# Differential attention with its scores in three banks, its output in two, and the memory keys and values moved behind it

## The chip, the cores and the metric

The kernel runs on one core of one Trainium2 chip. The metric is the device time of one execution in microseconds (us), less being better. TensorE (PE) multiplies, VectorE (DVE), ScalarE (ACT) and GpSimd (POOL) work on the results, and the queue of SyncE (SP) starts the weight loads. Every engine works through its own instructions in program order and waits on semaphores that the others raise.

## The reference, cut to what matters

Two transformer blocks on 512 tokens of width 1024. The change lies in the first block's mixer, which sums three gated branches:

```python
q_d, k_d, v_d, u_p, q_m, gate_logits = jnp.split(h @ w_in, split_pts, axis=-1)
# differential attention: 8 heads, two components of 64 each, blocks of 128 queries, causal
s = einsum(q, k) * scale + alibi_bias;  p = softmax(s)          # for each component c
a = p[:, :, 0] - lam * p[:, :, 1];      out = einsum(a, v)
y_attn = (rms_norm(out, subln_g) * (1 - lam_init)) @ w_attn_branch
y_pool = multiscale_pool(u_p, pool_w, pool_scale) @ w_pool_branch
k_m, v_m = split(rms_norm(mem, norm_mem) @ w_mem_kv)            # 256 memory tokens, 4 heads of 128
y_mem  = memory_cross_attention(q_m, k_m, v_m) @ w_mem_branch
mix = gates[0] * y_attn + gates[1] * y_pool + gates[2] * y_mem
```

## The kernel before

**Projections.** Every matrix product is done three times on PE, with weights and inputs each split into a high and a low part (`mm3`, L744; the instructions carry L747). Weights come in chunks of 512 KB through four places: SP loads a chunk, ACT rounds it (`act_round`, L687), POOL forms the rest (L728), and PE waits for that. A tile of 512 tokens with 8 contraction blocks is 24 matmuls, one with 4 blocks is 12.

**The differential stage** has 32 units, u = 4 e + i for head e and query block i, so unit u has (u mod 4) + 1 blocks of 128 keys. They go through the engines as a pipeline of steps s (`pe_diff`, `act_diff`, `dve_diff`). In step s:

- PE: the scores of unit s, a matmul for each of the two components (L1487); transposes of the combined probabilities of unit s-3 (L1495); the product with the values of unit s-4 into the output bank (L1503).
- DVE: the output of unit s-5, scaled (L1540); then for unit s-1 the bias and the maximum of each component (L1554), ahead of it at i = 0 a new scaling of the distances (L1551); then the combination of the two components of unit s-2 (L1562 to L1566).
- ACT: both exponentials of unit s-1 (L1515), the copy of the transposes of unit s-3 (L1523), the squares of unit s-6 (L1529).

The scores lie in four banks, two for each parity of s, so that the scores of unit s wait for the maxima of unit s-2. The output has one bank: the product of unit s-4 waits for the output of unit s-5 (`d_out(u - 1)`).

**Main work between the steps.** `weave` gives each engine, item by item, a piece of main work and then as many steps as are due by proportion; the pairing of items and steps is the same on all three engines. Main work is, in order: the gated pool branch `pg` (24 items: four times two gate tiles of two items each and two branch tiles of one item each), the memory queries `qm` (8 items), the normed memory `mem` (4 items, two transposed blocks each: PE L1637, ACT L1646, DVE L1658), the memory keys `km` (4) and the memory values `vm` (4). On DVE the item of a branch tile waits for that tile on PE and then runs L1598 and L1601; that of an even `qm` tile waits for the tile and copies it (L859). On ACT the item of a gate tile waits for it and runs a tanh, and the rounding of a later chunk stands behind it.

**Behind the stage** (`pe_branches`, `act_branches`, `dve_branches`): ACT takes roots (two table loads), DVE scales the 8 heads (L1753), PE does two gate tiles of `agt`; then PE turns the heads (L923, tiles `ao`) through two banks, ACT and DVE split them (L932, L942), and PE goes on with the branch tiles of `agt` and the memory attention.

Of the kernel before, what the change touches and what calls it, by code (L numbers as in the profile page):

```python
# [13 lines left out]
P = 128  # L14
# [150 lines left out]
def build(nc, a):  # L165
# [332 lines left out]
    d_scored = signal("d_scored", d_units)  # L498
    d_maxed = signal("d_maxed", d_units)
    d_exped = signal("d_exped", d_units)  # L500
# [56 lines left out]

    def in_ring(name, tiles, emptied, banks=(0, 1, 2, 3)):

        for u in range(tiles):  # L560
            b = banks[u % len(banks)]
# [909 lines left out]
    def d_bank(u, c):  # L1471
        return 2 + 2 * (u % 2) + c

    d_out_bank = bank(7, P)

    def pe_diff():
        PE.wait_ge(*freed_act("k", 7))
        PE.wait_ge(*freed_act("v", 15))
        PE.wait_ge(*mod_set(0, MOD_CHUNKS - 1))
        for s in range(N_D + 7):  # L1480
            if s < N_D:
                i, e, n = d_where(s)
                if s >= 2:
                    PE.wait_ge(*d_maxed(s - 2))
                for c in range(2):
                    part = slice(c * DIFF_DH, (c + 1) * DIFF_DH)
                    ins = PE.matmul(bank(d_bank(s, c), n), qT[part, e, i * P:(i + 1) * P], kT[part, e, 0:n])  # L1487
                ins.then_inc(*d_scored.by(s))
            if 0 <= s - 3 < N_D:
                u, (i, e, n) = s - 3, d_where(s - 3)  # L1490
                PE.wait_ge(*d_comb(u))
                if u >= 1:
                    PE.wait_ge(*d_copied(u - 1))
                for k in range(i + 1):
                    ins = PE.transpose(bank(6, P, k * P), sc2[u % 3][:, 0, k * P:(k + 1) * P], ident[:])  # L1495
                ins.then_inc(*d_turned.by(u))
            if 0 <= s - 4 < N_D:
                u, (i, e, n) = s - 4, d_where(s - 4)
                PE.wait_ge(*d_copied(u))
                if u >= 1:  # L1500
                    PE.wait_ge(*d_out(u - 1))
                for k in range(i + 1):
                    ins = PE.matmul(d_out_bank, aT[u % 2][:, k * P:(k + 1) * P], vt[:, k, e * P:(e + 1) * P],  # L1503
                                    start=k == 0, stop=k == i)
                ins.then_inc(*d_weighted.by(u))
            yield
# [143 lines left out]

    def dve_mem():
        DVE.wait_ge(*mixed("pg", 7))
        for b in range(CB):
            DVE.tensor_scalar(mdiag[:, b, :], ident[:], statistics("mem")[1][:, b:b + 1], None,
                              ALU.mult).then_inc(*diag.by("mem", b))
        for t in range(DT):
            DVE.wait_ge(*n_hi("mem", t))
# [4 lines left out]

    N_BESIDE_DIFF = 4 + 24 + 8 + 4 + 4 + 4

    def pe_beside_diff():
        yield from pe_gated_branch("pg", [(bhi, blo, SEQ)], 4, lambda: None, lambda n, k: PE.wait_ge(*pool_lo(k)))
        yield from pe_gemm("qm", X)
        yield from pe_mem()
        yield from pe_gemm("km", M, ready=lambda n, k: PE.wait_ge(*n_lo("mem", k)))
        yield from pe_gemm_tokens("vm", TOKENS["vm"])  # L1670

    def act_beside_diff():
        yield from act_gated_branch("pg")
        yield from act_copied("qm")
        yield from act_mem()
        yield from act_copied("km")
        yield from act_tokens("vm", vm)

    def dve_beside_diff():
        yield from dve_gated_branch("pg")  # L1680
        yield from dve_copied("qm")
        yield from dve_mem()
        yield from dve_copied("km")
        yield from dve_tokens("vm", vm)

    def pe_diff_stage():
        run(pe_pool())
        weave(pe_beside_diff(), pe_diff(), N_BESIDE_DIFF - 4, N_D + 7)

    def act_diff_stage():  # L1690
        run(act_pool())
        weave(act_beside_diff(), act_diff(), N_BESIDE_DIFF - 4, N_D + 7)

    def dve_diff_stage():
        for b in range(CB):
            DVE.wait_ge(*rstd("mem", b))
# [9 lines left out]
    def pe_branches():  # L1706
        def before(s):
# [7 lines left out]

        PE.wait_ge(*d_maxed(N_D - 1))
        PE.wait_ge(*d_copied(N_D - 1))
        at = pe_gated_branch("agt", [(ahi, alo, SEQ)], DT, lambda: pe_token_to_split(
            "ao", lambda t, k: qT[:, t, k * P:(k + 1) * P], DT, lambda t: head_scaled(t)),
            lambda n, k: PE.wait_ge(*ts_lo("ao", k)))  # L1720
# [3 lines left out]
        run(pe_gated_branch("mg", [(bhi, blo, SEQ)], 4, lambda: pe_token_to_split(  # L1724
            "om", lambda t, k: om[:, k, t * P:(t + 1) * P], MEM_HEADS, lambda t: attended("mem", 15)),
            lambda n, k: PE.wait_ge(*ts_lo("om", k))))

    def act_branches():
        ACTE.wait_ge(*d_squared(N_D - 1))
        ACTE.activation(hrms, hs, ACT.Sqrt, scale=1.0 / P, bias=eps).then_inc(*head_rms.by(0))  # L1730
        ACTE.preload_act_table(ACT.Exp)
        at = act_gated_branch("agt", before_branch=lambda: act_token_to_split("ao", ahi, DT, subg))
        for _ in range(5):
# [10 lines left out]

        run(act_gated_branch("mg", split, lambda: act_token_to_split("om", bhi, MEM_HEADS)))

    def dve_branches():
        DVE.wait_ge(*head_rms(0))
        dve_step(DVE.reciprocal(hs, hrms))
        dve_after()  # L1750
        for e in range(DIFF_HEADS):
# [3 lines left out]
        at = dve_gated_branch("agt", before_branch=lambda: dve_token_to_split("ao", ahi, alo, DT, subg))  # L1755
        for _ in range(5):
# [7 lines left out]

        run(dve_gated_branch("mg", split, lambda: dve_token_to_split("om", bhi, blo, MEM_HEADS)))

# [1169 lines left out]
```

## Time and profile before

| | us |
|---|---|
| median of three runs | 1913.64 (1910.06 to 1914.26) |
| profiled execution, its own time | 1917.37 |
| its span, first to last instruction | 1916.1 |
| PE busy | 1765.5 (92% of the span) |
| DVE, ACT, POOL busy | 1009.2, 744.4, 576.0 |
| mean granted TensorE clock | 0.962 |

The differential stage with its main work runs from about 206 to 403 us of the span, the turning of the heads from 412 to 421. Busy time is per engine; a number in square brackets behind a row is idle time of that engine just ahead of it, and what ended it.

### The profile page before, as it was taken

Reading aid. Unit: us, or ns where it says so; the run is one execution under the profiler, and the core shown is the slowest. Engines: PE = TensorE matmul, PEld = TensorE weight load, DVE = VectorE, ACT = ScalarE, POOL = GpSimd, SP = SyncE. Lnnn points to the kernel's source line nnn. Section 1 sums busy time; section 2 is a strip of 40 time slices with the busy share of each in tenths; the row PEclk is TensorE's granted clock in tenths of the full one; section 3 lists DMA queues with packets and bytes.
Section 4 is the critical chain, followed back from the end, with each engine's and each line's share of the span. In section 5 each row is a group of like instructions: output and inputs, shape, how many; then the busy total and the mean of one; then the engine's idle time right before and its main releaser. Section 6 shows DMA issues by size and latency. Waiting matters only on the chain.

```text
span 1916.1 us, 24709 instructions
## 1 busy us (share of the span) xinstructions
PE 1765.5 (92%) x9464; PEld 1408.1 (73%) x9464; DVE 1009.2 (53%) x2024; ACT 744.4 (39%) x1460; POOL 576.0 (30%) x257
## 2 busy tenths in 40 slices
PE   7999999889999899999998899898889979998887
PEld 5879767678888688887887676555568857885675
DVE  3678545542242533443787415566643577965533
ACT  4222344543233444444223341566633143224532
POOL 3566221253344044444343021100012224421131
PEclk9999999999999799999998799999999989999988
DMA  7456212132234133333653021000002423221021
GB/s 221 132 153 184 77 52 59 45 110 67 82 95 132 34 89 98 99 99 108 197 157 88 1 85 44 23 1 1 2 12 85 125 69 97 83 59 34 25 75 44
DMA packets 255363, 155.25 MB, mean 81 GB/s; under 512 B 5969, under 2 KB 250894, under 8 KB 255246
## 3 DMA queue, kind: packets, MB, share of 16 engines
q1 hardware_dynamic: 251998, 147.12, 26.2%
q10 hardware_dynamic: 3248, 6.55, 1.0%
q8 instruction: 76, 1.25, 0.3%
q14 instruction: 41, 0.34, 0.1%
HBM read 151.55 MB, written 2.10 MB: 80 GB/s over the span
## 4 chain that ended last, share of the span: by engine, by line
PE 81%; DVE 9%; ACT 5%; issue 3%; DMA 0%; DVEq 0%; SPq 0%; ACTq 0%
PE ps L747 64%; PE ps L2172 3%; PE ps L2161 3%; DVE mod_sums L1436 2%; PE ps L2191 2%; ACT probs L2245 2%; PE ps L960 1%; PE ps L1503 1%; PE ps L1451 1%; PE ps L1487 1%; PE ps L1015 1%; DVE probsT L2272 1%; DVE probs L2260 1%; DVE h_lo L1050 1%; ACT w_hi L687 1%
## 5 line engine op out<-in xcount | busy, mean ns | idle before, releaser
L728 POOL TENSOR_TENSOR w_lo<-w_raw,w_hi 128x1024 fp32r<-128x1024 f32 (+1 forms) x220 | 535.0, 2435 | 1263.6 <-ACT w_hi L687 1263.3
L747 PE MATMUL ps<-h_hi,w_lo 128*128 128x512 f32 x1088 | 440.3, 405 | 22.7 <-DVE h_lo L1050 9.7
L747 PE MATMUL ps<-h_lo,w_hi 128*128 128x512 f32 x1088 | 429.4, 395 | 0.0
L747 PE MATMUL ps<-h_hi,w_hi 128*128 128x512 f32 x1088 | 429.1, 394 | 0.0
L747 PEld LDWEIGHTS ps<-h_hi,w_lo 128*128 128x128 f32 x1088 | 207.6, 191 | 83.7 <-issue 19.2
L687 ACT ACTIVATE w_hi<-w_raw 128x1024 fp32r<-128x1024 f32 (+1 forms) x220 | 228.4, 1043 | 41.2 <-PE ps L747 34.4
L747 PEld LDWEIGHTS ps<-h_hi,w_hi 128*128 128x128 f32 x1088 | 207.7, 191 | 44.9
L747 PEld LDWEIGHTS ps<-h_lo,w_hi 128*128 128x128 f32 x1088 | 208.2, 191 | 42.0 <-issue 1.4
L1436 DVE SCALAR_TENSOR_TENSOR mod_sums<-mod_raw,small,mod_sums 128x256 f32<-128x256 f32 x336 | 182.9, 618 | 0.0
L2172 PE MATMUL ps<-ident,probs 128*128 128x128 f32 x528 | 86.6, 289 | 37.5 <-ACT probs L2245 15.6
L2172 PEld LDWEIGHTS ps<-ident,probs 128*128 128x128 f32 x528 | 56.8, 143 | 78.7 <-ACT probs L2245 31.8
L1881 DVE SCALAR_TENSOR_TENSOR conv<-ps,cols,conv 128x511 f32<-128x511 f32 x44 | 33.0, 750 | 125.3 <-ACT conv L1844 125.3
L2245 ACT ACTIVATE probs<-probs,small 128x512 f32<-128x512 f32 (+3 forms) x128 | 93.3, 729 | 12.0 <-DVE small L2260 9.0
L2234 ACT ACTIVATE probsT<-ps 128x256 f32<-128x256 f32 (+2 forms) x128 | 48.5, 379 | 106.7 <-PE ps L2172 106.5
L2632 DVE SCALAR_TENSOR_TENSOR ps<-u_T,cols,ps 128x512 f32<-128x512 f32 x116 | 76.8, 744 | 0.0
L747 PE MATMUL ps<-f_hi,w_lo 128*128 128x512 f32 x176 | 71.1, 404 | 4.6 <-DVE f_lo L1891 4.6
L747 PE MATMUL ps<-f_hi,w_hi 128*128 128x512 f32 x176 | 69.8, 397 | 0.0
L747 PE MATMUL ps<-f_lo,w_hi 128*128 128x512 f32 x176 | 69.3, 394 | 0.0
L1433 DVE SCALAR_TENSOR_TENSOR mod_sums<-mod_raw,small 128x256 f32<-128x256 f32 x48 | 59.8, 1285 | 7.0 <-DMA mod_raw<-in_mod_w 6.9
L2272 DVE COPY probsT<-ps 128x256 f32<-128x256 f32 (+2 forms) x128 | 55.8, 436 | 12.1 <-PE ps L2172 11.6
L747 PE MATMUL ps<-c_hi,w_lo 128*128 128x256 f32 x192 | 56.4, 293 | 1.7 <-DVE c_lo L1050 1.7
L747 PE MATMUL ps<-w_lo,h_hi 128*128 128x256 f32 x192 | 55.5, 289 | 0.6 <-POOL w_lo L728 0.6
(406 smaller groups left out, 3247.9 us busy)
## 6 DMA issues: line engine op xcount, KB each, us to landing
w_raw<-in_w_in SPq DMA_DIRECT2D x56, 512.0 KB, 6.4
mod_raw<-in_mod_w SPq DMA_DIRECT2D x24, 1024.0 KB, 5.2
w_raw<-in_w_up SPq DMA_DIRECT2D x44, 512.0 KB, 3.8
w_raw<-in_od_w_in SPq DMA_DIRECT2D x28, 512.0 KB, 3.8
w_raw<-in_ev_w_in SPq DMA_DIRECT2D x20, 512.0 KB, 3.8
w_raw<-in_w_down SPq DMA_DIRECT2D x16, 512.0 KB, 4.0
w_raw<-in_w_mem_kv SPq DMA_DIRECT2D x8, 512.0 KB, 4.0
w_raw<-in_w_attn_branch SPq DMA_DIRECT2D x8, 512.0 KB, 4.0
```

The source lines that it names most:

```text
L687: ACTE.activation(whi[:, p, 0:n], raw[:, p, 0:n], ACT.Copy).then_inc(*chunk_hi.by(c))
L728: POOL.tensor_tensor(wlo[:, p, 0:n], raw[:, p, 0:n], f(whi[:, p, 0:n]), ALU.subtract).then_inc(*chunk_lo.by(c))
L747: ins = PE.matmul(out, l, r, start=first and n == 0, stop=last and n == 2)
L1433: dve_step(DVE.scalar_tensor_tensor(out, w[:, k, :], c, zero1.to_broadcast([P, MOD_COLS]), ALU.mult, ALU.add))
L1436: ins = DVE.scalar_tensor_tensor(out, w[:, k, :], c, out, ALU.mult, ALU.add)
L2161: ins = PE.matmul(ps[:, pair_bank(s) * 512 + off:pair_bank(s) * 512 + off + w], u["q"][s], u["k"][s][:, at:at + w])
L2172: ins = PE.transpose(bank(b, P, k * P), probs[s][p % 2][:, at:at + P], ident[:])
L2191: PE.matmul(ps[s * HEAD:(s + 1) * HEAD, b * 512 + lo:b * 512 + hi], u0["v"](k, s), probsT[s][g % 2][:, k, lo:hi], start=n == 0, stop=n == ...
L2234: ACTE.activation(turned_to(probsT, p - 1, s, u["act"]), bank(5, w).rearrange("p (k n) -> p k n", n=P), ACT.Copy).then_inc(*p_copied_act.b ...
L2245: ins = ACTE.activation(S, S, ACT.Exp, bias=neg_max[:, s:s + 1], scale=-1.0, accum_out=total[:, s:s + 1])
L2272: DVE.tensor_copy(turned_to(probsT, p, s, part), bank(4, len(part) * P).rearrange("p (k n) -> p k n", n=P)).then_inc(*p_copied_dve.by(x_, ...
L2632: dve_step(DVE.scalar_tensor_tensor(so_far, src, wcol, so_far_, ALU.mult, ALU.add))
```

## The change

- The scores use three banks by component: component c of unit s lies in bank 2 + (2 s + c) mod 3. The scores of unit s wait for the maximum of component 0 of unit s-1 (the signal of the maxima now has an event for each component).
- The output uses two banks, 7 and 5 in turn; the product of a unit waits for the output two units before.
- DVE does the output of unit s-5 behind the maxima of unit s-1.
- `mem` is interleaved with `qm` (two items of `qm`, one of `mem`, four times), and `km` and `vm` leave the main work, which now has 36 items instead of 44 for the same 39 steps.
- Behind the stage PE does `km`, then `vm` with two head turns behind each tile, then `agt`. The turns go through four banks. ACT and DVE have their pieces in the matching order.

```diff
-    in_ring("qm", 4, by_table("qm"), TWO)
-    in_ring("mem", 8, lambda u: [n_lo("mem", u)], TWO)
+    for u in range(4):
+        in_ring("qm", 1, by_table("qm"), (u % 2,), u)
+        in_ring("mem", 2, lambda t: [n_lo("mem", t)], (1 - u % 2, u % 2), 2 * u)
-    in_ring("ao", 8, lambda u: [ts_lo("ao", u)], (2, 3))
+    in_ring("ao", 8, lambda u: [ts_lo("ao", u)], (2, 3, 4, 5))
...
     def d_bank(u, c):
-        return 2 + 2 * (u % 2) + c
-    d_out_bank = bank(7, P)
+        return 2 + (2 * u + c) % 3
+    def d_out_bank(u):
+        return bank((7, 5)[u % 2], P)
...
             if s < N_D:
-                if s >= 2:
-                    PE.wait_ge(*d_maxed(s - 2))
+                if s >= 1:
+                    PE.wait_ge(*d_maxed(s - 1, 0))
...
-                if u >= 1:
-                    PE.wait_ge(*d_out(u - 1))
+                if u >= 2:
+                    PE.wait_ge(*d_out(u - 2))
...
         for s in range(N_D + 7):
-            if 0 <= s - 5 < N_D:
-                u, (i, e, n) = s - 5, d_where(s - 5)
-                DVE.wait_ge(*d_weighted(u))
-                DVE.tensor_scalar(qT[:, e, i * P:(i + 1) * P], d_out_bank, d_stats(u)[:, 4:5], None,
-                                  ALU.mult).then_inc(*d_out.by(u))
             if 0 <= s - 1 < N_D:
...
-                ins.then_inc(*d_maxed.by(u))
+                    ins.then_inc(*d_maxed.by(u, c))
+            if 0 <= s - 5 < N_D:
+                u, (i, e, n) = s - 5, d_where(s - 5)
+                DVE.wait_ge(*d_weighted(u))
+                DVE.tensor_scalar(qT[:, e, i * P:(i + 1) * P], d_out_bank(u), d_stats(u)[:, 4:5], None,
+                                  ALU.mult).then_inc(*d_out.by(u))
...
-    N_BESIDE_DIFF = 4 + 24 + 8 + 4 + 4 + 4
+    N_BESIDE_DIFF = 24 + 8 + 4
+    def queries_and_memory(queries, memory):
+        for u in range(4):
+            next(queries)
+            yield
+            next(queries)
+            yield
+            next(memory)
+            yield
...
     def pe_beside_diff():
         yield from pe_gated_branch("pg", [(bhi, blo, SEQ)], 4, lambda: None, lambda n, k: PE.wait_ge(*pool_lo(k)))
-        yield from pe_gemm("qm", X)
-        yield from pe_mem()
-        yield from pe_gemm("km", M, ready=lambda n, k: PE.wait_ge(*n_lo("mem", k)))
-        yield from pe_gemm_tokens("vm", TOKENS["vm"])
+        yield from queries_and_memory(pe_gemm("qm", X), pe_mem())
...
-        weave(pe_beside_diff(), pe_diff(), N_BESIDE_DIFF - 4, N_D + 7)
+        weave(pe_beside_diff(), pe_diff(), N_BESIDE_DIFF, N_D + 7)
...
+        run(pe_gemm("km", M, ready=lambda n, k: PE.wait_ge(*n_lo("mem", k))))
+        turn = pe_token_to_split("ao", lambda t, k: qT[:, t, k * P:(k + 1) * P], DT, lambda t: head_scaled(t))
+        for _ in pe_gemm_tokens("vm", TOKENS["vm"]):
+            next(turn)
+            next(turn)
```

## Rows read from the trace of the kernel before

**Rows 1.** The page: busy us, share of the span, instructions.

```profile
PE 1765.5 (92%) x9464; PEld 1408.1 (73%) x9464; DVE 1009.2 (53%) x2024; ACT 744.4 (39%) x1460; POOL 576.0 (30%) x257
```

**Rows 2.** Stretches: us; PE, PEld, DVE, ACT, POOL busy; granted clock, DMA share, GB/s.

```profile
206.30:428.75 222.45, 203.81 (x1109) 155.32 (x1109) 109.01 (x321) 109.72 (x293) 68.13 (x29) 0.98 0.23 66
257.60:261.00 3.40, 3.40 (x11) 2.61 (x11) 1.78 (x7) 2.08 (x7) 0.00 (x0) 0.53 0.52 154
371.80:375.20 3.40, 3.40 (x26) 3.06 (x28) 0.65 (x3) 0.69 (x1) 2.39 (x1) 1.00 0.00 0
1718.60:1725.30 6.70, 5.53 (x16) 2.97 (x13) 2.32 (x7) 2.26 (x6) 0.27 (x1) 0.51 0.26 78
1851.70:1855.10 3.40, 3.40 (x9) 2.64 (x9) 0.24 (x1) 0.00 (x0) 2.37 (x1) 0.52 0.04 12
```

**Rows 3.** Waits of PE, 206.3 to 428.75: total us, times, longest.

```profile
PE ps L1503 <- DVE q_T L1540: 9.4, 9, 1.5
PE ps L923 <- DVE a_lo L942: 3.5, 3, 1.4
PE ps L1495 <- ACT diff_aT L1523: 2.0, 2, 1.0
```

**Rows 4.** Timeline of PE (start, us) around the end of a branch tile.

```profile
254.67 0.40 PE L747 MATMUL ps<-b_hi,w_hi 128*128 128x512 f32 x1
255.00 0.49 PE L1487 MATMUL ps<-k_T,q_T 64*128 64x128 f32 x4
...
257.39 0.46 PE L1503 MATMUL ps<-v_tok,diff_aT 128*128 128x128 f32 x2 [1.53 <-DVE q_T L1540]
```

**Rows 5.** Timeline of DVE behind the same tile and the next one.

```profile
255.11 0.69 DVE L1598 SCALAR_TENSOR_TENSOR gate_p<-gate_p,ps 128x512 f32<-128x512 f32 x1 [8.01 <-PE ps L747]
255.83 1.16 DVE L1601 TENSOR_SCALAR mix_T<-gate_p 128x512 f32<-128x512 f32 x1
256.91 0.34 DVE L1540 TENSOR_SCALAR q_T<-ps,small 128x128 f32<-128x128 f32 x1
257.17 0.68 DVE L1554 CUSTOM_DVE_ANT_0 diff_s<-ps,distance 128x512 f32<-128x512 f32 x1
...
263.57 0.48 DVE L1551 TENSOR_SCALAR distance<-distance,small 128x512 f32<-128x512 f32 x1
264.08 0.29 DVE L1554 CUSTOM_DVE_ANT_0 diff_s<-ps,distance 128x128 f32<-128x128 f32 x1
```

**Rows 6.** The chain that ended last: a branch tile (start, us).

```profile
239.76 2.75 PE ps L747 x12
```

**Rows 7.** Operations: count, ns min/median/max, first and last start.

```profile
L1601 DVE TENSOR_SCALAR mix_T<-gate_p x8: 426/792/2119, 230.1 to 319.6; 128x512 f32<-128x512 f32 x8
L859 DVE TENSOR_SCALAR qm_T<-ps x2: 691/692/692, 328.0 to 344.3; 128x512 f32<-128x512 f32 x2
L1646 ACT ACTIVATE m_hi<-ps,small,cols x8: 547/552/564, 356.8 to 371.0; 128x256 fp32r<-128x256 f32 x8
L1658 DVE SCALAR_TENSOR_TENSOR m_lo<-ps,cols,m_hi x8: 483/484/485, 357.4 to 371.6; 128x256 fp32r<-128x256 f32 x8
```

**Rows 8.** Groups by form, 212 to 429: busy us, mean ns; idle before.

```profile
L728 POOL TENSOR_TENSOR w_lo<-w_raw,w_hi 128x1024 fp32r<-128x1024 f32 x28 | 67.1, 2404 | 152.8 <-ACT w_hi L687 152.6
L687 ACT ACTIVATE w_hi<-w_raw 128x1024 fp32r<-128x1024 f32 x28 | 29.3, 1051 | 2.9 <-PE ps L747 2.9
L1515 ACT ACTIVATE diff_s<-diff_s,small 128x384 f32<-128x384 f32 x16 | 9.7, 607 | 15.8 <-DVE small L1554 15.8
```

**Rows 9.** Timeline of PE: the last memory item, the first of km.

```profile
368.94 1.06 PE L1637 MATMUL ps<-m_diag,mem_in 128*128 128x128 f32 x8
371.70 0.35 PE L747 MATMUL ps<-m_hi,w_lo 128*128 128x256 f32 x1 [1.71 <-issue]
```

**Rows 10.** Timeline of PE: the gaps ahead of the last two stretches.

```profile
1717.19 0.65 PE L2172 MATMUL ps<-ident,probs 128*128 128x128 f32 x4 [2.12 <-ACT probs L2245]
1851.45 0.51 PE L747 MATMUL ps<-o_hi,w_lo 128*128 128x512 f32 x1 [1.82 <-DVE o_lo L2797]
```

More of the change, by code:

```diff
@@ L498, in build @@
     d_scored = signal("d_scored", d_units)
-    d_maxed = signal("d_maxed", d_units)
+    d_maxed = signal("d_maxed", [(u, c) for u in d_units for c in range(2)])
     d_exped = signal("d_exped", d_units)
@@ L556, in build, with in_ring @@
     BANK, BEFORE, EMPTIED, holder = {}, {}, {}, {}
-    def in_ring(name, tiles, emptied, banks=(0, 1, 2, 3)):
-        for u in range(tiles):
-            b = banks[u % len(banks)]
+    def in_ring(name, tiles, emptied, banks=(0, 1, 2, 3), first=0):
+        for u in range(first, first + tiles):
+            b = banks[(u - first) % len(banks)]
             BANK[name, u], BEFORE[name, u] = b, holder.get(b)
@@ L1499, in pe_diff @@
                 PE.wait_ge(*d_copied(u))
-                if u >= 1:
-                    PE.wait_ge(*d_out(u - 1))
+                if u >= 2:
+                    PE.wait_ge(*d_out(u - 2))
                 for k in range(i + 1):
-                    ins = PE.matmul(d_out_bank, aT[u % 2][:, k * P:(k + 1) * P], vt[:, k, e * P:(e + 1) * P],
+                    ins = PE.matmul(d_out_bank(u), aT[u % 2][:, k * P:(k + 1) * P], vt[:, k, e * P:(e + 1) * P],
                                     start=k == 0, stop=k == i)
@@ L1655, in dve_mem @@
                               ALU.mult).then_inc(*diag.by("mem", b))
+    def dve_mem():
         for t in range(DT):
@@ L1661, in dve_mem @@
                 yield
-    N_BESIDE_DIFF = 4 + 24 + 8 + 4 + 4 + 4
+    N_BESIDE_DIFF = 24 + 8 + 4
+    def queries_and_memory(queries, memory):
+        for u in range(4):
+            next(queries)
+            yield
+            next(queries)
+            yield
+            next(memory)
+            yield
+        assert next(queries, None) is None and next(memory, None) is None
     def pe_beside_diff():
         yield from pe_gated_branch("pg", [(bhi, blo, SEQ)], 4, lambda: None, lambda n, k: PE.wait_ge(*pool_lo(k)))
-        yield from pe_gemm("qm", X)
-        yield from pe_mem()
-        yield from pe_gemm("km", M, ready=lambda n, k: PE.wait_ge(*n_lo("mem", k)))
-        yield from pe_gemm_tokens("vm", TOKENS["vm"])
+        yield from queries_and_memory(pe_gemm("qm", X), pe_mem())
     def act_beside_diff():
         yield from act_gated_branch("pg")
[L1674 to L1677, printed above, removed]
+        ACTE.wait_ge(*tile_done("pg", 15))
+        yield from queries_and_memory(act_copied("qm"), act_mem())
     def dve_beside_diff():
         yield from dve_gated_branch("pg")
[L1681 to L1684, printed above, removed]
+        dve_mem_diag()
+        yield from queries_and_memory(dve_copied("qm"), dve_mem())
     def pe_diff_stage():
         run(pe_pool())
-        weave(pe_beside_diff(), pe_diff(), N_BESIDE_DIFF - 4, N_D + 7)
+        weave(pe_beside_diff(), pe_diff(), N_BESIDE_DIFF, N_D + 7)
     def act_diff_stage():
         run(act_pool())
-        weave(act_beside_diff(), act_diff(), N_BESIDE_DIFF - 4, N_D + 7)
+        weave(act_beside_diff(), act_diff(), N_BESIDE_DIFF, N_D + 7)
     def dve_diff_stage():
@@ L1723, in pe_branches @@
         weave(at, pe_attention("mem", mem_units, mprobs, mprobsT, before), 27, 20)
-        run(pe_gated_branch("mg", [(bhi, blo, SEQ)], 4, lambda: pe_token_to_split(
-            "om", lambda t, k: om[:, k, t * P:(t + 1) * P], MEM_HEADS, lambda t: attended("mem", 15)),
+        run(pe_gated_branch("mg", [(bhi, blo, SEQ)], 4, lambda: run(pe_token_to_split(
+            "om", lambda t, k: om[:, k, t * P:(t + 1) * P], MEM_HEADS, lambda t: attended("mem", 15))),
             lambda n, k: PE.wait_ge(*ts_lo("om", k))))
@@ L1731, in act_branches @@
         ACTE.preload_act_table(ACT.Exp)
-        at = act_gated_branch("agt", before_branch=lambda: act_token_to_split("ao", ahi, DT, subg))
+        run(act_copied("km"))
+        split = act_token_to_split("ao", ahi, DT, subg)
+        for _ in act_tokens("vm", vm):
+            next(split)
+            next(split)
+        at = act_gated_branch("agt")
         for _ in range(5):
@@ L1743, in split @@
                 ACTE.activation(ahi[:, t, :], mixT[:, t, :], ACT.Copy).then_inc(*mx_hi.by(t))
-        run(act_gated_branch("mg", split, lambda: act_token_to_split("om", bhi, MEM_HEADS)))
+        run(act_gated_branch("mg", split, lambda: run(act_token_to_split("om", bhi, MEM_HEADS))))
     def dve_branches():
@@ L1750, in dve_branches @@
         dve_after()
+        keys = dve_copied("km")
         for e in range(DIFF_HEADS):
@@ L1754, in dve_branches @@
                               ALU.mult).then_inc(*head_scaled.by(e))
-        at = dve_gated_branch("agt", before_branch=lambda: dve_token_to_split("ao", ahi, alo, DT, subg))
+            if e % 2:
+                next(keys)
+        split = dve_token_to_split("ao", ahi, alo, DT, subg)
+        for _ in dve_tokens("vm", vm):
+            next(split)
+            next(split)
+        at = dve_gated_branch("agt")
         for _ in range(5):
@@ L1763, in split @@
             DVE.tensor_tensor(alo[:, t, :], mixT[:, t, :], f(ahi[:, t, :]), ALU.subtract).then_inc(*mx_lo.by(t))
-        run(dve_gated_branch("mg", split, lambda: dve_token_to_split("om", bhi, blo, MEM_HEADS)))
+        run(dve_gated_branch("mg", split, lambda: run(dve_token_to_split("om", bhi, blo, MEM_HEADS))))
     def pe_mix():
```

13 lines of the change are left out of this document (5 added, 8 removed).

## The prediction

> **What bounds the kernel now.** The page first: PE is busy 92% of the span, no other engine more than 53% [rows 1]. Another engine's time matters only where PE stands still for it, or where such standing makes PE's clock fall. The change adds and removes almost no PE instruction, so the question is what becomes of PE's idle time in the stretch that it touches. That stretch, 206.3 to 428.75 us (pool products to the first memory scores), has 222.45 us with 203.81 busy, thus 18.6 idle [rows 2], of which 1.9 belong to the pool products, which the change leaves alone. Next the waits of PE: 9.4 us in nine waits of the value product (L1503) for the output step, 2.0 of the transposes for ACT's copy, 3.5 for the split of the turned heads [rows 3], and 1.7 ahead of the first `km` matmul [rows 9]; sum 16.6 us.
>
> How a wait of the first kind arises is seen at one branch tile. Its last matmul ends at 255.07; PE does the scores and the transposes and then stands 1.53 us for the output [rows 4]. DVE had to take the branch tile first: L1598 from 255.11, L1601 from 255.83, the output from 256.91, ended at 257.25, and PE starts 0.14 later [rows 4, 5]. The scores and transposes, some 0.8 us here, cover part of DVE's delay. And the first maximum of the unit scored one step earlier starts only at 257.17 [rows 5], over 2 us after PE has begun to score the next unit at 255.00. Before, nobody minds: the scores wait for the unit two back. The gap is followed by a clock of 0.53 for 3.4 us, the 1.2 GHz level, against 1.00, the 2.4 GHz level, elsewhere [rows 2]. Such a stretch under a busy PE costs half its length, 1.7 us. The 0.98 over the whole 222 us [rows 2] is two of them, together 3.4 us.
>
> **What the change removes.** The output wait, by two banks: 9.4 us. ACT's late copy, 2.0, which stands behind late maxima and moves into the terms below. The turned heads wait, 1.4 at the longest [rows 3], because two banks are filled, split and freed in turn; with four banks and a `vm` tile behind every second head (24 matmuls of half width, so the 2.75 us of 12 full ones [rows 6]) they wait no more: 3.5. The 1.7 ahead of `km` go into a new term. With the two slow stretches, 16.6 + 3.4 = 20.0 us are taken out, and all that comes back is counted anew.
>
> **What it adds: the scores wait for unit s-1.** With three banks, the scores of s need component 0 of s-1 out of its bank. That maximum is in DVE's step s, behind DVE's main item; PE's scores of s are the very first thing behind PE's main item. Where DVE's main item waits for the tile that PE has just ended (all eight branch tiles, `qm` 0), nothing of PE's covers DVE's way: 0.04 to start, 0.72 from L1598 to the next, L1601, the maximum, 0.14 back to PE [rows 4, 5]. L1601 lasts 0.43 at the least and 2.1 at the most [rows 7]: 0.35 to the next instruction for the second tile of each pair, about 1.5 for the first, over which POOL's 2.4 us operation on a weight chunk lies [rows 8]. Nothing in the change moves that chunk from there, so I keep 1.5. The maximum lasts 0.29 for 128 keys and 0.68 for 512 [rows 5], about 0.42 and 0.55 between. At i = 0 scaling the distances adds 0.51 [rows 5].
>
> Pairing 36 items with 39 steps, item n (from 0) has step floor(39(n+1)/36) - 1 as its last. First tiles are items 4, 10, 16, 22 with steps 4, 10, 17, 23, so the maxima are of units 3 (512 keys), 9 (256), 16 (128 and the scaling), 22 (384): gaps of 3.1, 2.8, 3.2, 3.0. Second tiles, items 5, 11, 17, 23 (units 4, 10, 17, 23): 2.1, 1.8, 1.7, 1.9. Sum 19.6 us. Items 11 and 23 have two steps at once: for unit 11 DVE must do maximum, output and combination (about 1.6 us) and another 0.68 and 0.14, against 2.2 us of work on PE: 0.2; for unit 24 it needs 2.9 against 1.1: 1.8. Together 2.0.
>
> At gate items DVE waits for nothing of PE's main item, and a gate half has 2.75 us of matmuls in which the maximum gets done: no gap. At `qm` 0 the copy takes 0.69 [rows 7] (0.60 to the next), the maximum 0.55, the ends 0.18: 1.3 us. At `qm` 2 no scores are left.
>
> **Memory items.** Two have scores behind them (items 26 and 29). PE's own work in one is 1.06 us [rows 9]; then ACT has to do two m_hi of 0.55 and DVE the last m_lo of 0.48 [rows 7] ahead of the maximum. ACT comes late besides: for the first it has two exponentials of 0.6 [rows 8] behind DVE's copy of `qm` 0, for the second its own copy of `qm` 1, the rounding of 1.05 [rows 8] and two exponentials. Followed through, PE stands 1.9 and 2.7 us. The third costs 0.3 (combination of unit 31). Ahead of `km`, in place of the 1.7, the last m_lo pair comes behind `qm` 3's copy, a rounding and squares on ACT: 2.2. For `km` and `vm` PE has eight times 2.75, 22 us of matmuls, which hide the roots, two table loads and the head scaling; if they did not, that is if DVE freed the bank of `km` 0 late, 1 us more. One weight chunk of `vm` is 0.8 late. Sum of these: 7.9 us.
>
> All new gaps: 19.6 + 2.0 + 1.3 + 7.9 = 30.8 us, against 16.6 removed: 14.2 more.
>
> **The clock.** The trace of before shows gaps on both sides of the point where the clock falls: after 1.71 it stays [rows 2, 9], after 1.53 and 1.82 it falls for 3.4 us, after 2.12 for 6.7 [rows 2, 4, 10]. Of the new gaps eleven places have between 1.7 and 3.2 us, ten of them 1.8 or more. Bounds: none falls, 0; each falls for 6.7 us, 11 x 3.4 = 37 us. I take ten falls of 3.4 us, most of it under a busy PE, 1.6 us each: 16, less the 3.4 there are now: 12.6. The rows with gaps of 1.8 and more are nearest, and there the clock fell.
>
> The Trainium skill weighs this otherwise: its page "TensorE: Matmul & The Clock Gate", section "Why this matters for your kernels", lets only gaps longer than nearly all of those forecast here drop the clock. This case's trace disagrees, by the gaps of 1.53 and 1.82. By that rule the sum would lack the whole term of 16; what the time would be without it is the first rival.
>
> **Sum.** 14.2 + 12.6 = 26.8 us. The profiled execution took 1917.4 (span 1916.1 and 1.3 around it), so it would be near 1944; that run lies 3.7 above the median of 1913.6. On the median: 1940.
>
> **Rivals.**
> - The clock holds: new gaps as above, hardly a fall: 14.2 - 3.4 = 10.8, time 1924. For it: the gap of 1.71 that left it at 1.00, and only two falls from the waits of [rows 3]. Against: the rows of 1.53 and up.
> - The falls run together, as after the 2.12 gap, or L1601 of the first tiles takes its 2.1 each time: 12 to 15 us more, 1954.
> - Faster: the maxima are in time. If DVE came to component 0 before PE's main item ends at branch tiles and `qm` 0, the 19.6, 2.0 and 1.3 would be nothing, and with them nearly all falls of the clock: 7.9 - 20.0 = -12, time 1902. It decides when the scores' waits at these items average below 0.5 us. For it: at all gate items DVE is early. Against: the maximum that starts at 257.17 [rows 5] belongs to the unit that this wait would ask for at 255.0; output first or second changes 0.27 us of this.
> - The two waits balance: PE pays at the scores what it paid at the product, no change. It needs gaps at branch tiles no longer than the 1.5 at most of now, though the scores and transposes that covered them come to stand behind the wait.
>
> **How the numbers follow.** Main case 0.64 (1931 to 1948 by itself, five to thirteen falls), clock holds 0.15, falls run together 0.11, balance 0.04, faster 0.06. About 0.2%, 3.8 us, is what a measurement of this kernel can tell from no change. Leaving out balance, faster and the outer tails: 1921 to 1954. Slower 0.90, same 0.04, faster 0.06.
>
> **What would show it.** In the profile after: PE's wait at L1487 for DVE's maxima (L1554), some twelve times and 20 to 28 us in total, near zero now; L1503's wait for L1540 gone; no wait at L923; gaps of about 3 us behind first branch tiles and 2 us behind second ones; a granted clock of the stage clearly below the 0.98 of [rows 2]. I am wrong if the scores' waits sum to under 10 us, or if the clock stays at 1.00 after gaps of 2 to 3 us.

## The result, and the profile after

The changed kernel takes 1935.25 us (median of four runs, 1928.92 to 1940.59) against 1913.95 (four runs beside it, 1910.06 to 1916.74). The ratio is 1.0107, with a 95% interval from 1.0086 to 1.0127: slower by 21.3 us. (The ratios here and below are the recorded ones with their intervals; the quotient of two medians comes out 0.0003 to 0.0008 higher, less than half an interval.) Forecast were 1940 (1921 to 1954) and slower with a chance of 0.90. The profiled run took 1940.59 us with a span of 1939.2, which is 23.1 more than before. It is the slowest of the four, 5.3 us above their median, as the profiled run of before was 3.4 above its own, so the profiles overstate the difference by some 2 us.

In this kernel L1492 are the scores, L1500 the transposes, L1508 the product with the values, L1554 the maxima, L1551 the scaling of the distances, L1571 the combination, L1603 and L1606 the two operations of a branch tile, L748 the matmuls and L729 POOL's operation.

The page's row of busy time, which answers to [rows 1]. The amount of work is the same:

```profile
PE 1776.3 (92%) x9464; PEld 1417.4 (73%) x9464; DVE 1017.9 (52%) x2024; ACT 745.7 (38%) x1460; POOL 574.0 (30%) x257
```

The waits of PE from 206 to 446 us (total us, times, longest), which answer to [rows 3]:

```profile
PE ps L1492 <- DVE small L1554: 26.7, 12, 4.1
PE ps L748 <- DVE m_lo L1664: 1.6, 1, 1.6
PE ps L748 <- POOL w_lo L729: 1.2, 1, 1.2
PE ps L1620 <- DVE b_lo L1633: 1.0, 1, 1.0
PE ps L748 <- DVE b_lo L1633: 0.9, 1, 0.9
PE ps L1500 <- DVE diff_s L1571: 0.5, 1, 0.5
PE ps L1642 <- ACT qm_T L853: 0.3, 1, 0.3
```

The product's wait for the output and the turned heads' wait for their split are gone. In their place the scores wait twelve times for the maxima. The two waits for b_lo belong to the pool products and were there before.

The stretches (us; PE, PEld, DVE, ACT and POOL busy; granted clock, DMA share, GB/s), which answer to [rows 2]. The first is the whole stage. It starts, as in [rows 2], 0.76 us ahead of the first pool product and ends at the first memory scores. The others are single places in it.

```profile
208.03:450.85 242.82, 210.57 (x1110) 161.40 (x1110) 116.79 (x321) 110.73 (x293) 69.43 (x29) 0.94 0.21 60
234.60:241.30 6.70, 5.62 (x18) 4.52 (x19) 2.55 (x8) 1.79 (x5) 0.14 (x1) 0.52 0.37 112
244.90:248.20 3.30, 3.30 (x14) 2.91 (x13) 2.58 (x10) 2.00 (x8) 0.00 (x0) 0.53 0.00 0
272.20:275.50 3.30, 3.30 (x14) 2.86 (x12) 0.00 (x0) 1.02 (x5) 0.00 (x0) 0.53 0.37 111
279.20:282.60 3.40, 3.40 (x22) 2.31 (x23) 3.29 (x13) 2.31 (x8) 0.00 (x0) 1.00 0.00 0
306.30:313.00 6.70, 5.73 (x19) 4.40 (x20) 2.39 (x9) 1.66 (x7) 0.30 (x1) 0.52 0.32 93
342.00:345.40 3.40, 3.40 (x21) 2.41 (x18) 1.08 (x6) 1.76 (x7) 0.00 (x0) 1.00 0.51 149
350.70:354.00 3.30, 2.89 (x12) 2.24 (x13) 2.93 (x15) 2.15 (x10) 0.00 (x0) 0.53 0.02 5
368.10:371.50 3.40, 3.40 (x19) 2.84 (x20) 3.23 (x15) 2.73 (x10) 0.00 (x0) 1.00 0.00 0
381.40:384.70 3.30, 3.17 (x10) 1.67 (x11) 2.21 (x11) 1.87 (x7) 0.00 (x0) 0.54 0.54 162
```

The stage is 242.82 us long instead of 222.45, so 20.4 more. Its idle time is 242.82 - 210.57 = 32.25 instead of 18.64 (13.6 more), and its busy time 210.57 instead of 203.81 (6.8 more). The stage also starts 1.7 us later (the first pool product is at 208.79 instead of 207.06). That shift lies ahead of the change: it was 0.7 to 2.6 us in the experiments. Behind the stage 1.0 us is left of the 23.1. Six times the clock falls to the 1.2 GHz level, for some 27 us together instead of 6.8.

The timeline of PE at every wait of over 1 us from the first branch tile on (start, us; in brackets the idle time ahead of it):

```profile
235.68 0.80 PE L1492 MATMUL ps<-k_T,q_T 64*128 64x128 f32 x4 [3.23 <-DVE small L1554]
244.25 0.70 PE L1492 MATMUL ps<-k_T,q_T 64*128 64x256 f32 x4 [1.97 <-DVE small L1554]
270.92 0.92 PE L1492 MATMUL ps<-k_T,q_T 64*128 64x384 f32 x4 [2.74 <-DVE small L1554]
279.18 1.13 PE L1492 MATMUL ps<-k_T,q_T 64*128 64x512 f32 x4 [1.72 <-DVE small L1554]
307.27 1.22 PE L1492 MATMUL ps<-k_T,q_T 64*128 64x256 f32 x4 [4.05 <-DVE small L1554]
316.05 0.92 PE L1492 MATMUL ps<-k_T,q_T 64*128 64x384 f32 x4 [1.58 <-DVE small L1554]
341.63 1.13 PE L1492 MATMUL ps<-k_T,q_T 64*128 64x512 f32 x4 [2.71 <-DVE small L1554]
348.52 0.49 PE L1492 MATMUL ps<-k_T,q_T 64*128 64x128 f32 x4 [1.85 <-DVE small L1554]
351.11 1.23 PE L1492 MATMUL ps<-k_T,q_T 64*128 64x256 f32 x4 [1.50 <-DVE small L1554]
363.12 1.13 PE L1492 MATMUL ps<-k_T,q_T 64*128 64x512 f32 x4 [1.26 <-DVE small L1554]
368.08 0.49 PE L1492 MATMUL ps<-k_T,q_T 64*128 64x128 f32 x4 [1.79 <-DVE small L1554]
381.53 2.01 PE L1492 MATMUL ps<-k_T,q_T 64*128 64x512 f32 x4 [2.29 <-DVE small L1554]
404.34 0.35 PE L748 MATMUL ps<-m_hi,w_lo 128*128 128x256 f32 x1 [1.64 <-DVE m_lo L1664]
417.10 0.38 PE L748 MATMUL ps<-w_lo,m_hi 128*128 128x256 f32 x1 [1.22 <-POOL w_lo L729]
```

The first eight are the eight branch tiles in order, followed by the second step at one of them (351.11), `qm` 0 (363.12) and the two memory items that have scores behind them. The longest gap, 4.05 us, is at the third first tile. There DVE (first fence) and POOL (second) did this:

```profile
303.25 0.69 DVE L1603 SCALAR_TENSOR_TENSOR gate_p<-gate_p,ps 128x512 f32<-128x512 f32 x1 [4.77 <-PE ps L748]
303.97 0.43 DVE L1606 TENSOR_SCALAR mix_T<-gate_p 128x512 f32<-128x512 f32 x1
304.32 2.56 DVE L1551 TENSOR_SCALAR distance<-distance,small 128x512 f32<-128x512 f32 x1
306.91 0.29 DVE L1554 CUSTOM_DVE_ANT_0 diff_s<-ps,distance 128x128 f32<-128x128 f32 x1
```

```profile
301.15 2.41 POOL L729 TENSOR_TENSOR w_lo<-w_raw,w_hi 128x1024 fp32r<-128x1024 f32 x1 [7.41 <-ACT w_hi L688]
304.06 2.53 POOL L729 TENSOR_TENSOR w_lo<-w_raw,w_hi 128x1024 fp32r<-128x1024 f32 x1 [0.50 <-ACT w_hi L688]
```

L1606 began 0.09 us ahead of POOL's second operation and took 0.43. The scaling behind it came under the second one and took 2.56 instead of the 0.48 of [rows 5].

### The profile page after: what moved, and what is told of

The parts are those of the page before. It is cut to its first block, busy times and chain, and to the rows that moved or that the text cites. A ratio compares the mean times of both kernels' runs of the same rounds, so it can differ in the third digit from the quotient of the medians.

```text
span 1939.2 us, 24707 instructions
## 1 busy us (share of the span) xinstructions
PE 1776.3 (92%) x9464; PEld 1417.4 (73%) x9464; DVE 1017.9 (52%) x2024; ACT 745.7 (38%) x1460; POOL 574.0 (30%) x257
## 3 DMA queue, kind: packets, MB, share of 16 engines
q8 instruction: 76, 1.25, 0.3%
## 4 chain that ended last, share of the span: by engine, by line
PE 81%; DVE 10%; ACT 5%; issue 3%; POOL 0%; DMA 0%; DVEq 0%; SPq 0%; ACTq 0%
PE ps L748 63%; PE ps L2197 3%; PE ps L2186 3%; DVE mod_sums L1440 3%; PE ps L2216 2%; ACT probs L2270 2%; PE ps L1492 1%; PE ps L964 1%; PE ps L1508 1%; PE ps L1455 1%; DVE probsT L2297 1%; PE ps L1019 1%; PE ps L1500 1%; DVE probs L2285 1%; DVE h_lo L1054 1%
## 5 line engine op out<-in xcount | busy, mean ns | idle before, releaser
L729 POOL TENSOR_TENSOR w_lo<-w_raw,w_hi 128x1024 fp32r<-128x1024 f32 (+1 forms) x220 | 533.0, 2426 | 1290.4 <-ACT w_hi L688 1290.3
L748 PE MATMUL ps<-h_hi,w_lo 128*128 128x512 f32 x1088 | 442.6, 407 | 22.2 <-DVE h_lo L1054 9.7
L748 PE MATMUL ps<-h_lo,w_hi 128*128 128x512 f32 x1088 | 431.2, 396 | 0.0
L748 PE MATMUL ps<-h_hi,w_hi 128*128 128x512 f32 x1088 | 430.5, 396 | 0.0
L748 PEld LDWEIGHTS ps<-h_hi,w_lo 128*128 128x128 f32 x1088 | 208.8, 192 | 83.6 <-issue 19.7
L748 PEld LDWEIGHTS ps<-h_hi,w_hi 128*128 128x128 f32 x1088 | 208.8, 192 | 45.5
L748 PEld LDWEIGHTS ps<-h_lo,w_hi 128*128 128x128 f32 x1088 | 209.4, 192 | 41.9 <-issue 1.4
L748 PE MATMUL ps<-f_hi,w_lo 128*128 128x512 f32 x176 | 70.7, 401 | 4.6 <-DVE f_lo L1916 4.6
L748 PE MATMUL ps<-f_hi,w_hi 128*128 128x512 f32 x176 | 69.7, 396 | 0.0
L748 PE MATMUL ps<-f_lo,w_hi 128*128 128x512 f32 x176 | 69.3, 394 | 0.0
L2297 DVE COPY probsT<-ps 128x256 f32<-128x256 f32 (+2 forms) x128 | 55.8, 436 | 12.1 <-PE ps L2197 11.6
L748 PE MATMUL ps<-c_hi,w_lo 128*128 128x256 f32 x192 | 56.5, 294 | 2.1 <-DVE c_lo L1054 1.9
L748 PE MATMUL ps<-c_hi,w_hi 128*128 128x256 f32 x192 | 55.5, 289 | 0.0
```

Source lines behind the costliest of these rows:

```text
L729: POOL.tensor_tensor(wlo[:, p, 0:n], raw[:, p, 0:n], f(whi[:, p, 0:n]), ALU.subtract).then_inc(*chunk_lo.by(c))
L748: ins = PE.matmul(out, l, r, start=first and n == 0, stop=last and n == 2)
L2297: DVE.tensor_copy(turned_to(probsT, p, s, part), bank(4, len(part) * P).rearrange("p (k n) -> p k n", n=P)).then_inc(*p_copied_dve.by(x_, ...
```

## The experiments

Eight kernels ran. Every ratio is against the kernel before on the same chip, whose median was 1917.39 us (13 runs) beside the first four and 1915.68 (19 runs) beside the last four. "The stage" is the time from the first pool product to the first memory scores, in the profiled run. It was 221.7 us before and 242.1 after.

| | what it is | median | ratio, 95% | stage | scores' waits |
|---|---|---|---|---|---|
| e1 | after, with the old banks and order | 1917.44 | 0.9993, 0.9982 to 1.0004 | 220.5 | 0.7 |
| e2 | before, with the new banks and order | 1937.34 | 1.0096, 1.0081 to 1.0111 | 239.2 | 27.1 |
| e3 | after, maxima of unit s in step s | 1903.81 | 0.9925, 0.9909 to 0.9942 | 207.0 | 3.9 |
| e4 | after, gaps filled with matmuls | 1928.45 | 1.0051, 1.0033 to 1.0069 | 230.5 | 8.8 |
| e5 | after, L1606 behind the maxima | 1924.11 | 1.0036, 1.0022 to 1.0050 | 228.6 | 19.0 |
| e6 | before, maxima of unit s in step s | 1914.56 | 0.9990, 0.9976 to 1.0004 | 219.0 | none |
| e7 | e2, maxima of unit s in step s | 1905.61 | 0.9940, 0.9921 to 0.9960 | 211.6 | 1.0 |
| e8 | e3, scaling ahead of its step | 1902.01 | 0.9926, 0.9911 to 0.9941 | 208.0 | 3.0 |

### e1 and e2: which half of the change costs

The change has two halves that don't need each other: the banks with their waits and DVE's order, and the moved memory work with the four-bank head turns. e1 takes the banks out of the kernel after. e2 puts them alone into the kernel before. This is e1's edit against the kernel after; the step's output in DVE also goes ahead of the maxima again. e2's edit against the kernel before is its reverse.

```diff
-        return 2 + (2 * u + c) % 3
+        return 2 + 2 * (u % 2) + c
...
-                if s >= 1:
-                    PE.wait_ge(*d_maxed(s - 1, 0))
+                if s >= 2:
+                    PE.wait_ge(*d_maxed(s - 2, 1))
...
-                if u >= 2:
-                    PE.wait_ge(*d_out(u - 2))
+                if u >= 1:
+                    PE.wait_ge(*d_out(u - 1))
```

> The changed kernel with its four old score banks, its one output bank and the output ahead of the maxima; the interleaved memory items and the keys and values behind the attention stay. Theory A (the scores' wait for the unit just before is the cost): the 26.7 us of PE's waits at the scores are gone, the waits of the value product for the output come back with 9 to 12 us, the turned heads don't wait; time 1905 to 1917, at or a little below the kernel before. Rival B (the moved memory work costs the time, by its late chunks and its chain through ACT and DVE): the time stays at 1925 or more, with the waits at the memory items and ahead of km and vm.

> The kernel before with only the banks changed: scores through three banks, two output banks, output behind the maxima; the memory work stays where it was. Theory A: waits at the scores of 22 to 32 us in total behind the eight branch tiles, two memory query tiles and four memory items, the output waits of 9.4 us gone, four to nine stretches of low clock in the stage; time 1928 to 1942. Rival B: 1917 or less, since the banks remove a wait.

Measured: e1 is level with before (0.9993) and e2 has the loss (1.0096, where the whole change has 1.0107). The waits of PE from 206 to 446 us, first of e1 (L1507 is the product, L1544 the output), then of e2 (L1488 are the scores, L1550 the maxima):

```profile
PE ps L1507 <- DVE q_T L1544: 8.8, 10, 1.6
```

```profile
PE ps L1488 <- DVE small L1550: 27.1, 13, 3.4
PE ps L923 <- DVE a_lo L942: 3.2, 3, 1.4
```

With the old banks the old output wait is back and the scores hardly wait (0.7). With the new banks alone the scores wait 27.1 us and the turned heads still 3.2. So the loss is the scores' wait, and the moved memory work, which by itself is no gain that these runs can tell, is not its cause. In e1's profile it takes away the 3.5 us of the turned heads, puts 1.6 ahead of `km` and 1.6 ahead of a weight chunk of `vm`, and the transposes wait 3.3 us for ACT's copy where it was 2.0 before. The place of the output on DVE, behind the maxima or ahead of them, was moved together with the banks in both kernels, so its own share isn't shown.

### e3: the same banks, the maxima one step earlier

Theory: nothing but DVE's order makes the scores late. In step s the scores of unit s wait for a maximum that DVE takes in its own step s, behind its main item. If DVE does the maxima of unit s last in step s, they are done ahead of the next main item, on which it waits for PE anyway. The body of the maxima is moved whole, from the head of the step to its end.

```diff
         for s in range(N_D + 7):
-            if 0 <= s - 1 < N_D:
-                u, (i, e, n) = s - 1, d_where(s - 1)
...
             if 0 <= s - 5 < N_D:
...
             if 0 <= s - 2 < N_D:
...
+            if s < N_D:
+                u, (i, e, n) = s, d_where(s)
...
             yield
```

> The changed kernel with one thing moved on DVE: in step s it does the maxima of unit s, last in the step, in place of those of unit s-1, so they stand ahead of the next main item. Theory A (only DVE's order makes the scores wait): scores' waits under 4 us in total, idle time of PE in the stage 5 to 10 us in place of 30, at most two stretches of low clock there; time 1895 to 1905, faster than the kernel before. Rival C (DVE's way is simply too long for this pipeline, and the wait goes elsewhere, to the combination or the output): waits of 10 us or more at the transposes or products, time 1912 or more.

Measured: 1903.81, ratio 0.9925, below both kernels. The waits of PE, and the whole stage in the columns of the stretches above:

```profile
PE ps L1492 <- DVE small L1569: 3.9, 4, 2.2
```

```profile
208.93:416.67 207.74, 198.14 (x1110) 152.77 (x1109) 116.36 (x321) 109.92 (x293) 69.67 (x29) 1.00 0.24 71
```

The clock is 1.00 throughout, PE idles for 9.6 us instead of 32.25, and it is busy for 198.14 us instead of 210.57, with the same number of matmuls. DVE's timeline at the first branch tile shows the order (L1569 are now the maxima):

```profile
230.72 0.69 DVE L1569 CUSTOM_DVE_ANT_0 diff_s<-ps,distance 128x512 f32<-128x512 f32 x1 [2.49 <-PE ps L1500]
...
233.38 0.69 DVE L1603 SCALAR_TENSOR_TENSOR gate_p<-gate_p,ps 128x512 f32<-128x512 f32 x1 [1.35 <-PE ps L748]
234.10 1.88 DVE L1606 TENSOR_SCALAR mix_T<-gate_p 128x512 f32<-128x512 f32 x1
```

PE begins the next scores at 233.28. The maximum that they need was begun at 230.72, in time in which DVE would have waited for the tile. L1606 takes as long as ever and nobody waits for it here.

### e4: what of the loss is clock

Theory: part of the loss isn't the gaps themselves but the clock behind them. e4 keeps PE at work in the gaps with 103 matmuls of 384 columns, put ahead of the scores' wait; their results go to a free part of an output bank and are read by nobody. The wait for the output that the next product into this bank needs anyway is put ahead of them.

```diff
+    FILL = {4: 13, 10: 13, 17: 13, 23: 13, 5: 7, 11: 7, 18: 7, 24: 7, 25: 7, 27: 4, 28: 4, 31: 8}
...
+                if s in FILL and s >= 6:
+                    PE.wait_ge(*d_out(s - 6))
+                for _ in range(FILL.get(s, 0)):
+                    PE.matmul(ps[:, (7, 5)[s % 2] * 512 + P:(7, 5)[s % 2] * 512 + 512], hhi[:, 0, 0:P], hhi[:, 0, 0:3 * P])
                 if s >= 1:
                     PE.wait_ge(*d_maxed(s - 1, 0))
```

> The changed kernel with useless matmuls of 384 columns on PE ahead of the scores that wait: 13 at the four first branch tiles, 4 to 8 at the eight other places, 17 us in total, less than the gaps. They write columns that nobody reads. Theory A (the low clock behind the gaps costs some 10 us of the 21): the low clock in the stage goes from 27.3 us to under 10, scores' waits from 26.7 to about 9, the rest unchanged; time 1924 to 1930. Rival D (the clock term is nothing, the gaps alone are the loss): no change against the changed kernel, 1935, or more where a filler is longer than its gap.

Measured: 1928.45, ratio 1.0051. The stage, and PE at the first of the filled gaps (the first line shows the last nine of its thirteen useless matmuls):

```profile
208.88:440.13 231.25, 216.45 (x1212) 170.29 (x1212) 116.59 (x321) 110.58 (x293) 70.13 (x29) 1.00 0.22 64
```

```profile
233.82 1.73 PE L1493 MATMUL ps<-h_hi 128*128 128x384 f32 x9
236.58 0.49 PE L1498 MATMUL ps<-k_T,q_T 64*128 64x128 f32 x4 [1.03 <-DVE small L1560]
```

The useless matmuls cost 216.45 - 198.14 = 18.3 us (against the busy time of e3), and 8.8 of waiting is left. Together that is 27.1, as long as the 26.7 of gaps in the kernel after. The clock stays at 1.00 and the stage is 11.6 us shorter. So with the same delay at the scores, a clock that doesn't fall is worth 11.6 us in the profile and 1.0107 - 1.0051, some 10.7 us, in the times. With the intervals of the two ratios the latter is good to 5 us or so.

### e5: L1606 out of the way

Theory: each gap is a sum of DVE's operations, with L1606 as one term. e5 halves the tile only behind the maxima of the step, so the term should vanish from the branch gaps and from nothing else. The rival: DVE is late for another reason, and the gaps stay.

```diff
             if job == "pg":
-                ins = DVE.tensor_scalar(mixT[:, fm, :], g, 0.5, None, ALU.mult)
+                later.append((fm, g))
+                return
...
                     ins.then_inc(*d_maxed.by(u, c))
+            while later:
+                fm, g = later.pop()
+                DVE.tensor_scalar(mixT[:, fm, :], g, 0.5, None, ALU.mult).then_inc(*mixed.by("pg", fm))
```

> The changed kernel with one DVE operation per branch tile moved: the halved product (the operation that took 1.4 to 1.8 us behind first branch tiles and 0.43 behind second ones) comes behind the maxima of the step, not ahead of them. Theory A (the gap is DVE's way from tile to maximum, term by term): the eight gaps at branch tiles shrink by 1.3 us each at three of the first and 0.35 at the others, scores' waits from 26.7 to about 20; with fewer low-clock stretches time 1926 to 1932 where the changed kernel has 1935. Rival E (GpSimd's operation holds up whatever DVE does there next, the scaling of the distances or the maximum, so that moving one operation wins nothing): waits of 25 or more, 1935.

Measured: 1924.11, ratio 1.0036. The first five gaps at branch tiles:

```profile
234.61 0.49 PE L1492 MATMUL ps<-k_T,q_T 64*128 64x128 f32 x4 [1.51 <-DVE small L1556]
240.10 0.70 PE L1492 MATMUL ps<-k_T,q_T 64*128 64x256 f32 x4 [1.64 <-DVE small L1556]
263.67 0.92 PE L1492 MATMUL ps<-k_T,q_T 64*128 64x384 f32 x4 [1.25 <-DVE small L1556]
269.99 1.13 PE L1492 MATMUL ps<-k_T,q_T 64*128 64x512 f32 x4 [1.38 <-DVE small L1556]
295.88 0.70 PE L1492 MATMUL ps<-k_T,q_T 64*128 64x256 f32 x4 [1.63 <-DVE small L1556]
```

3.23, 1.97, 2.74 and 1.72 became 1.51, 1.64, 1.25 and 1.38. The first tiles lose the long L1606, the second tiles its 0.35. At the third first tile 4.05 became 1.63, a gain of 2.4 us where the theory had 0.35. Without L1606 ahead of it the scaling began at 295.01, 0.09 us before POOL's operation, and took 0.49; the halving, now behind the maxima, was held up in its place (2.05 us) and nobody waited for it. So the largest single gain came from a tenth of a microsecond in POOL's start. The recorded rival, that POOL holds up whatever comes next, is refuted for the maximum: at the first tile it ran at 233.86 under POOL's pair of operations (230.67 to 235.40) and took its usual 0.69. For the scaling this run doesn't test it. All eight gaps sum to 11.6 instead of 19.9 us; two other waits grew by 0.3 each. The scores' waits sum to 19.0 instead of 26.7, and the stage is 13.5 us shorter. The other 5.8 are nearly all less busy time of PE (204.78 instead of 210.57 us): the clock falls three times instead of six. It stayed at 1.00 behind all five of these gaps.

### e6, e7 and e8: which parts of e3 are needed

e6 puts e3's order into the kernel before. e7 puts it into e2, so that it has the new banks but the memory work where it was. Their diffs move the same body as e3's. e8 is e3 with the scaling of the distances moved from the head of a step i = 0 to behind the last maxima of the step before; this is its edit against e3.

```diff
-                if i == 0:
+                if s == 0:
                     dve_step(DVE.tensor_scalar(dist[:], dist[:], slopes[:, 0:1], None, ALU.mult))
                     dve_after()
+                elif i == 0:
+                    DVE.wait_ge(dve_chain, scaled[0])
...
+                if i == NB - 1 and s < N_D - 1:
+                    DVE.wait_ge(*d_maxed(u, 1))
+                    dve_step(DVE.tensor_scalar(dist[:], dist[:], slopes[:, 0:1], None, ALU.mult))
+                    scaled[0] = chained["dve"]
```

> The kernel before, four score banks and one output bank, with the maxima of unit s in DVE's step s, last in the step. Theory A (the second output bank is what removes the output wait, early maxima alone don't): the waits for the output stay at 7 to 10 us, the waits for ACT's late copy (2.0) go; time 0 to 4 us below the kernel before. Rival F (early maxima are the whole gain of the version with both, the banks are not needed): output waits under 3 us, time 8 us or more below the kernel before.

> The kernel before with the new banks and the maxima of unit s in DVE's step s, but all memory work where it was. It prices the move of the memory work where the scores don't wait. Theory A: scores' waits 2 to 5 us, the heads' turns wait 3.5 us again, the four memory items wait for DVE or ACT 2 to 4 us; 4 to 8 us slower than the version that moves the memory work too (ratio 0.9925), that is 0.994 to 0.997 of the kernel before. If the moved memory work is worth nothing, the ratio is 0.992 to 0.993.

> The version with the maxima of unit s in step s, and besides the scaling of the distances for the next head moved behind the last maxima of a head. Theory A: of the 3.9 us that the scores still wait, the part with the scaling (0.7 to 2.2 us at heads' first units) goes, 1 to 3 us less; ratio to the kernel before 0.991 to 0.992. If the waits there come from the two steps at once and not from the scaling, no change: 0.9925.

Measured: e6 0.9990, no difference that can be told. Its wait of PE shows why:

```profile
PE ps L1503 <- DVE q_T L1540: 8.0, 9, 1.5
```

With one output bank the product waits for the output as before, and with four score banks no scores waited for the maxima anyway. In the profile the transposes' 2.0 us of waiting for ACT is gone, and 2.1 us ahead of the first memory item, which waits for DVE's `m_diag`, are new. The order needs the banks, and the banks need the order.

e7 has 0.9940 and e3 0.9925. The intervals overlap, so what the moved memory work adds is not settled by the times. In the profile e7's stage is 4.6 us longer than e3's. It still has 3.3 us of waits of the turned heads and one of 2.1 ahead of the first memory item, the same as in e6, and 10.2 us at the low clock where e3 has none.

e8 has 0.9926, the same as e3. The scores' waits fall from 3.9 to 3.0 us only, so the scaling is a small part of what is left. More than half of the 3.0 is one wait of 1.68, ahead of the second of the two steps that follow one item (2.20 in e3).

## Why the prediction was right

**The mechanism and the place.** The scores' waits were forecast at some twelve places with 20 to 28 us; there are twelve with 26.7. e1 and e2 show that they carry the loss, and e3 that DVE's order makes them. The removed waits (L1503, L923, the transposes' for ACT) are gone as said.

**The gaps, one by one.** Forecast for the eight branch tiles in order were 3.1, 2.1, 2.8, 1.8, 3.2, 1.7, 3.0, 1.9; measured are 3.23, 1.97, 2.74, 1.72, 4.05, 1.58, 2.71, 1.85. The sum is 19.85 against 19.6; it comes this close partly by luck, since 0.85 too much at one tile stands against small shortfalls at six others. The double step (1.8) is 1.50, `qm` 0 (1.3) is 1.26, the memory items (1.9 and 2.7) are 1.79 and 2.29. What was off:

- The gap of 4.05 (3.2 forecast). I let POOL's operation lie over L1606 at each first tile. Here it lay over the scaling right behind it, which I had priced at its undisturbed 0.51. The delay was 2.1 us instead of L1606's 1.1 or so. Which of two operations gets it is decided by some tenths of a microsecond of POOL's start.
- The 0.2 at unit 11's double step: no wait shows there.
- Ahead of `km` 2.2, measured 1.64. The weight chunk of `vm` 0.8, measured 1.22. The 0.3 of the third memory item is 0.5, and 0.3 of waiting for ACT's copy of `qm` came unforecast.

In total the stage's idle time grew by 13.6 us, where 14.2 was forecast.

**The clock: the term that was mis-sized.** "I take ten falls of 3.4 us" gave 16, less the 3.4 of before, thus 12.6. There were six falls, two of them 6.7 us long. The busy time of PE in these six stretches is 24.0 us, of which the low clock costs half, 12.0. Two other readings agree: e4 gives 11.6, and the stage of e3 at full clock has 12.4 us less busy time. So the gross term was 12, not 16. The net was 6.8 by the busy times, not 12.6. By the 3.4 of before it should be near 8.6; the other 1.8 are not accounted for (before's 203.81 us are 5.7 above e3's 198.14, and two falls explain 3.4 of that). The missing 5.8 of the net are nearly the whole distance of the forecast sum of 26.8 from the 20.4 of the stage.

What failed in that term was the step from "there the clock fell" to a fall behind each of ten gaps. It stayed at 1.00 behind 2.71 (the stretch at 342.00), and it fell behind 1.97 and 2.29. It also stayed behind 1.72 and 1.79 (the stretches at 279.20 and 368.10), which is where the forecast had its bound. The price of 1.6 us a fall was low: these six cost 2.0 each, since two lasted 6.7 us. The working also counts eleven places with gaps of 1.7 us or more where its own list has twelve, unless units 23 and 24 are taken as one. My own sign of being wrong, a clock that stays after gaps of 2 to 3 us, came true once, while six falls came as the main case wanted (five to thirteen). The first rival, no falls, is out by the six falls. What it says of a held clock is borne out by e4, whose stage lost 8.8 us to before (the rival had 10.8), where the kernel after lost 20.4.

Before's second fall, which the prediction names without a place, is this stretch:

```profile
363.90:367.30 3.40, 3.40 (x16) 2.97 (x16) 2.16 (x9) 2.56 (x9) 0.00 (x0) 0.54 0.00 0
```

It stands behind waits of 1.05 and 1.46 us (PE starts again at 361.80 and 363.77), shorter than the 1.53 that the prediction took as the shortest.

How long the clock is low also differs between executions of one kernel. Of before's 19 runs the fastest (1912.47) was granted 0.965 on average over the whole kernel and the slowest (1920.53) 0.960; of the four of the kernel after, 1928.92 had 0.960 and 1940.59 had 0.956. The counts of falls here are those of one execution each, and e3's profile, without a fall in the stage, has the highest mean clock of its four runs (0.965; the others 0.961 to 0.964). So part of the distance between ten falls and six is luck, and how large a part isn't shown.

The rule of the Trainium skill that was weighed against the trace ("TensorE: Matmul & The Clock Gate", "Why this matters for your kernels"), that only longer gaps of PE drop the clock, is contradicted again by the falls behind 1.97 and 2.29 us.

**The other rivals.** That the maxima are in time was refuted by the waits. It took e3's order to make it true, and then the kernel was 13.6 us faster than before (1903.81 against 1917.39), near the 12 worked out for that rival. Balance was refuted by the waits of the kernel after and of e2 (26.7 and 27.1 us at the scores, 9.4 at the product before). Falls that run together happened at two of the eight branch tiles, not throughout.

## What to carry to other kernels

Before a buffer ring is made shorter on one side to give a bank to the other, list for each consumer where in its program the freeing operation stands, relative to the item on which both engines meet. A wait for the unit one back is free only if the freeing engine does it ahead of that item. Here the banks cost 1.0 to 1.1% with the maxima behind the item (e2, after) and gained 0.6 to 0.8% with the same operations ahead of it (e7, e3). When an engine has idle time just before such an item, put there what others wait for first, and leave behind it what nobody needs soon.

## What the runs showed of the hardware

**The length of a gap alone doesn't tell whether the clock falls.** It fell behind gaps of 1.46 (after one of 1.05), 1.53 [rows 4], 1.97 and 2.29 us, and not behind gaps of 1.71 [rows 9], 1.72, 1.79 and 2.71. In e5 it held behind the five gaps of 1.25 to 1.64 shown. What else decides was not tried. A forecast with such a term needs both bounds in its range, no fall and a fall behind every gap.

**POOL holds up an operation of DVE until it ends.** POOL's operation on a weight chunk ended at 306.59 and DVE's scaling, begun under it at 304.32, at 306.88. An operation of DVE that began first was not held up: L1606 at 303.97, with POOL's operation following at 304.06, took 0.43, and e5's scaling at 295.01, with POOL's at 295.10, took 0.49. At the three other first tiles of the kernel after, the L1606 begun under such an operation ended 0.27 to 0.28 us behind it too (durations 1.81, 1.58 and 1.42 instead of 0.43). L1603, which has the matmul's bank as one of its inputs, wasn't held up: at 232.49 it lay wholly under POOL's pair of operations (230.02 to 234.74) and took its usual 0.69. The Trainium skill ("SBUF — State Buffer", "SBUF: two separate sides") says that DVE and GpSimd share a pair of ports, which whichever starts first holds for a whole instruction while the other blocks, and that on DVE's side this holds for operations in a two-port mode or with two inputs in SBUF. The trace agrees: the delay is what is left of POOL's operation, not a share of its speed, and L1603 with one input in PSUM goes free. Which mode L1606 and the scaling ran in no run here shows.
